# The sums of an expert pass moved from between the gate and the up product to behind the up product

## The reference

```python
def expert_block(args):
    xb, e = args
    h = jax.nn.silu(xb @ w_gate[e]) * (xb @ w_up[e])     # (rows, 1024) @ (1024, 512), twice
    return h @ w_down[e]                                  # (rows, 512) @ (512, 1024)
...
ys = lax.map(expert_block, (xs, blk_exp)).reshape(R, dm)
out = jax.ops.segment_sum(ys * row_w[:, None].astype(ys.dtype), row_tok, num_segments=T + 1)[:T]
x = x + out
```

## Time and profile before

| | |
|---|---|
| median of three runs | 1389.87 us (1386.5 to 1400.7) |
| profiled execution | 1389.18 us, its span 1387.4 us |
| TensorE busy, matmul | 1125.7 us, 81% |
| VectorE, ScalarE, GpSimd busy | 474.2, 174.4 and 22.9 us |
| chain that ended last | TensorE 48%, transfers 41%, VectorE 7% |
| expert stage of layer 0 | 246.6 to 695.3 us |
| expert stage of layer 1 | 922.5 to 1382.9 us |
| mean granted clock of TensorE | 0.905 |

### The profile page before, as it was taken

One profiled execution on the slowest core, in us unless ns is written; L12 is line 12 of the kernel. 1 busy time (PEld: TensorE's weight loads), 2 busy tenths in 40 slices (PEclk: granted clock), 3 DMA queues, 4 the chain that ended last, 5 costly groups with the idle time before them and its releaser, 6 DMA issues.

```text
span 1387.4 us, 23289 instructions
## 1 busy us (share of the span) xinstructions
PE 1125.7 (81%) x9552; PEld 611.2 (44%) x9553; DVE 474.2 (34%) x1245; ACT 174.4 (13%) x415; POOL 22.9 (2%) x35
## 2 busy tenths in 40 slices
PE   5998889998987667777789896999666777779956
PEld 3475545444443333333357564544333333334433
DVE  0873533332232211222158635143221222213311
ACT  2312201010000000000032231100000000000100
POOL 3000000100000000000000000000000000000000
PEclk9998979999999988898999896999988888989988
DMA  9611433889999999999963324339999999995995
GB/s 315 223 62 61 182 121 124 329 359 428 428 428 429 428 428 429 428 428 429 404 246 125 122 69 182 136 141 427 428 428 429 428 428 429 428 428 232 429 429 249
DMA packets 49338, 439.73 MB, mean 317 GB/s; under 512 B 9200, under 2 KB 11408, under 8 KB 24720
## 3 DMA queue, kind: packets, MB, share of 16 engines
q1 hardware_dynamic: 47232, 435.79, 76.1%
q0 software_dynamic: 960, 1.51, 0.6%
q10 hardware_dynamic: 1104, 1.85, 0.4%
HBM read 437.56 MB, written 1.05 MB: 316 GB/s over the span
## 4 chain that ended last, share of the span: by engine, by line
PE 48%; DMA 41%; DVE 7%; issue 2%; DVEq 1%; ACT 1%; ACTq 0%; SPq 0%
DMA ring<-in_e_w_up_dram 19%; DMA ring<-in_e_w_gate_dram 16%; PE PS L1367 12%; PE PS L1415 6%; PE PS L1395 5%; DMA ring<-in_e_w_down_dram 5%; PE PS L1659 4%; PE PS L1339 3%; PE PS L1330 3%; PE PS L1409 2%; PE PS L1349 2%; PE PS L1587 1%; PE PS L1589 1%; PE PS L1678 1%; DMA gT<-in_norm_g_dram 1%
## 5 line engine op out<-in xcount | busy, mean ns | idle before, releaser
L1367 PE MATMUL PS<-ring,hT 128*32 128x256 f32 x4608 | 335.7, 451 | 172.1 <-DMA ring<-in_e_w_gate_dram 120.2
L1367 PEld LDWEIGHTS PS<-ring,hT 128*32 128x32 f32 x4608 | 184.7, 125 | 346.3 <-issue 285.1
L1395 PE MATMUL PS<-ring,hT 128*32 128x512 f32 x1152 | 137.2, 618 | 17.5 <-DMA ring<-in_e_w_down_dram 16.3
L795 DVE TENSOR_SCALAR hT<-hT 128x256 f32<-128x256 f32 x36 | 10.6, 294 | 335.7 <-ACT hT L558 335.7
L1415 PE MATMUL PS<-ring,hT 128*128 128x512 f32 x256 | 121.8, 630 | 0.0
L1339 PE MATMUL PS<-cst,mixT 64*64 64x64 f32 x1216 | 81.6, 283 | 4.5
L1339 PEld LDWEIGHTS PS<-cst,mixT 64*64 64x64 f32 x1216 | 77.4, 213 | 13.5 <-issue 12.0
L1349 PE MATMUL PS<-hT 64*128 64x512 f32 x304 | 75.5, 615 | 1.4 <-ACT hT L563 1.4
L1395 PEld LDWEIGHTS PS<-ring,hT 128*32 128x32 f32 x1152 | 37.4, 113 | 87.9 <-issue 86.4
L1415 PEld LDWEIGHTS PS<-ring,hT 128*128 128x128 f32 x256 | 50.4, 203 | 58.4 <-issue 58.1
L1330 PE MATMUL PS<-xres,scr 128*64 128x512 f32 x304 | 73.6, 605 | 1.8 <-DVE scr L778 1.8
(11 more groups left out here) (335 smaller groups left out, 974.2 us busy)
## 6 DMA issues: line engine op xcount, KB each, us to landing
ring<-in_e_w_gate_dram SPq DMA_DIRECT2D x64, 2048.0 KB, 34.8
ring<-in_e_w_up_dram SPq DMA_DIRECT2D x64, 2048.0 KB, 32.9
ring<-in_e_w_down_dram SPq DMA_DIRECT2D x64, 2048.0 KB, 35.0
ring<-in_w_in_dram SPq DMA_DIRECT2D x10, 2048.0 KB, 18.4
ring<-in_w_out_dram SPq DMA_DIRECT2D x2, 4096.0 KB, 13.6
ring<-in_w_in_dram SPq DMA_DIRECT2D x2, 1024.0 KB, 25.3
xres<-in_x_dram ACTq DMA_DIRECT2D x1, 1024.0 KB, 10.8
out_dram<-xres SPq DMA_DIRECT2D x1, 1024.0 KB, 4.0
```

Source lines behind the costliest of these rows:

```text
L1367: last = pe.matmul(PS[o:o + UT, bank, 0:256], xTe[:, k, UT * u:UT * u + UT], w[u][:, k, :, 2 * h:2 * h + 2], start=k == 0, stop=k == KD - 1)
L1395: last = pe.matmul(PS[o:o + UT, 3, :], hTe[:, c % 2, hc:hc + UT], w[u][:, c, 512 * h:512 * h + 512], start=c == 0, stop=c == KF - 1)
```

## The change

The two lines `combine(n, False)` and `in_product(1, 2)` change places in `one_pass` of TensorE. C is issued behind U and ahead of the gather, in every one of the 36 passes. No other engine's program changes.

```diff
@@ -1370,8 +1370,8 @@
 
                 pe.wait_ge(s_xte, n + 1)
                 in_product(0, 1)
+                in_product(1, 2)
                 combine(n, False)
-                in_product(1, 2)
                 pe.wait_ge(s_hit, n + 1)
                 gather(s_gath)
                 pe.wait_ge(s_h, n + 1)
```

## The result

The changed kernel takes 1393.76 us (median of 20 runs, 1390.01 to 1402.49), the kernel before 1388.20 (median of 20). The ratio is 1.0036 with a 95% interval of 1.0018 to 1.0053: some 5 us slower. Predicted were 1394 and +4.9 us.

A forecast was written before the change was run, and what follows sets the result against it. The prediction took expert weight transfers at 428 GB/s as the bound, with slack on TensorE. Layer 0's end 2.27, layer 1's pause 0.70 and its end 1.92 gave +4.9 us on 1389.18: 1394, range 1388 to 1400.

The forecast's parts named there:

- The bound and the slack: Expert stages: weight transfers at 428 GB/s set the pace; shifts inside transfer-paced passes away from an end are worth 0.
- Release of the up tiles: Up product ends 1.92 us sooner where tiles are there, but both pauses end at a gate product: worth 0.
- Passes with tiles in place: Passes whose tiles are all there: TensorE's work keeps its sum of 17.7 us and nothing is late: worth 0.
- The clock: Up products behind longer bare waits for tiles run partly at 1.2 GHz: taken at 5.36 us, nearly each one slow.
- End of layer 0: Last pass of layer 0: slow up product, then bare combining, start the down product later: +2.27 us.
- End of layer 1: Last pass of layer 1: up product already slow, down product follows without a wait, so combining adds +1.92 us.
- The pause of layer 1: First pass of the twelfth pair, ahead of the transfers' pause: next gate product starts later, +0.70 us.
- The sum: Whole kernel: 2.27 + 0.70 + 1.92 = +4.9 us on a profiled execution of 1389.18 us.
- A (clock no worse): Rival: up products come out no slower by the clock, +1.7 down to -0.9 us, 1388.3 to 1390.9; chance 0.18.
- B: Rival: sooner release of the up tiles shortens the two pauses, at most 1.92 us each, 1390; chance 0.03.
- C: Rival: weight queue runs dry in every pair, 21 gate waits grow, 40 us (1430) or 73 us (1462); chance 0.04.
- D: Rival: the exchange shows nowhere, since the down product waits for its tiles anyway, 1389; chance 0.02.

The follow-up runs named there:

- the block behind U: Changed kernel with four more float32 matmuls of 512 columns behind the combining in every pass, timed against the kernel before: ratio 1.0239, +33 us.
- the wait filled: Changed kernel with seven float32 matmuls of 256 columns between gate and up products in each layer's last pair, against the kernel before: ratio 1.0037.

## Why the prediction was right

**The bound and the slack.** Right. The transfers run on at their rate, each pass takes the late D out of its wait for the gate, and with C behind U in 22 passes the last U's come 0.3 us sooner and 0.6 later than in the mean of before.

**Release of the up tiles, worth 0.** Right. The two pauses in the changed kernel, SP's issues (start, us until the last of the row):

```profile
269.87 20.51 SPq L469 DMA_DIRECT2D ring<-in_e_w_up_dram  x2
...
1224.99 49.37 SPq L469 DMA_DIRECT2D ring<-in_e_w_up_dram  x2
```

They end at 290.38 and 1274.36, again behind the last G of the pair, which began at 286.06 and 1270.05.

**Passes with tiles in place, worth 0.** Right but for some 0.15 us: G and U side by side take less than apart. They stand in one row of 128 matmuls, and the passes follow each other after 17.54 us (17.70 in the earlier trace rows):

```profile
268.52 7.43 PE L1367 MATMUL PS<-ring,hT 128*32 128x256 f32 x128
...
286.06 7.43 PE L1367 MATMUL PS<-ring,hT 128*32 128x256 f32 x128
```

**The clock.** The rule from the rows held: 73 of the 75 U's that waited in the three changed traces were slow; the two quick ones had waited 2.01 and 2.30 us. The line is not sharp: over the traces of before U's behind 2.04 us were slow and one behind 2.44 was quick, and with C behind U in 22 passes one behind 3.93 us was quick. No D was slow in the changed kernel (4, 6 and 7 of 36 before).

The Trainium skill ("TensorE: Matmul & The Clock Gate", "HAM oscillation — how this bites in real kernels") tells this of a kernel whose waits for transfers last some 3 to 5 us: behind each of them the next block starts at the low clock. The slow U's behind 3 us and more in the changed traces agree. The prediction took it for waits of any length, and so read more into it than it states. In the three traces of before 74 U's waited for their tiles: the 37 with 1.99 us or less were all quick, and of the 37 with 2.02 us or more 32 were slow, 27 of them behind 2.04 to 2.76 us, which is shorter than the waits that the skill tells of.

**End of layer 0.** +2.27 stood there; means of three 12.35 against 9.78 us: +2.57.

**End of layer 1.** +1.92; 12.40 against 10.28: +2.12. The trace that I had read was the slow one of three (11.17 us from U to D, against 9.71 and 9.97, where U took 3.88 and 5.25), so the U of 6.45 us that I had kept as it was is partly a loss of the change. By what mattered the two ends are alike, C and the slower U; where C was moved in the last pair alone they cost 3.3 and 2.8 us over the means.

**The pause of layer 1.** The one mis-sized term: +0.70. From the U of the first pass to the next G it was 14.84, 14.76 and 13.33 us before, 15.21, 16.67 and 16.57 after: +1.84, and +1.81 up to the last U of the stage. I had put U at 5.36 us; in two of three it took 6.47 and 6.58. The second trace of the changed kernel:

```profile
1234.01 6.58 PE L1367 MATMUL PS<-ring,hT 128*32 128x256 f32 x64 [5.93 <-DMA ring<-in_e_w_up_dram]
...
1247.23 3.64 PE L1395 MATMUL PS<-ring,hT 128*32 128x512 f32 x32
1250.68 7.43 PE L1367 MATMUL PS<-ring,hT 128*32 128x256 f32 x128
```

Its G had been quick (3.85 us), so the wait to the tiles, which come 9.8 us after G's start, was the longer: the time that a quick G saves, U pays. I had also counted the D of 4.95 us as always slow; in the third trace of before it took 3.43.

**The sum.** +4.9 predicted; the stages of three traces each give +6.8 (2.6 + 2.1 + 1.8, and 0.3 up to the last U of layer 0, where one changed trace lost 1.2 us), the medians +5.6, the ratio +5.0. That the forecast of the median came so near has some luck in it: one term was too small, and the rest of the program scatters more than the error.

**Rivals.** A (clock no worse) fell with the slow U's, B with the pauses that end at a gate product, C with the block behind U, which cost 23 us and not 76, D with U to D.

## What to carry to other kernels

Work that an engine does while it waits for a transfer is free only on that side of the wait. To price moving it, look not at the passes in the middle, which take it in, but at the last pass of each stage and at the passes ahead of each place where the queue of transfers runs empty. A longer idle time of TensorE has a second price, the products behind it at the low clock, and moving the idle time elsewhere moves that price along: it should stand ahead of the product that the end depends on least. And cut traces at the stages before comparing totals: here the parts that nothing touched scattered by more than the effect.

## What the runs showed of the hardware

The stretch ahead of the first G took from 244.06 to 250.94 us over thirteen traces, the one between the stages 230.02 to 237.28, with the same instructions. The same 25 us of the mixer part of layer 0, first in the kernel before, then in the changed one (windows as above):

```profile
140.00:165.00 25.00, 22.66 (x120) 15.90 (x118) 13.98 (x28) 9.89 (x34) 0.00 (x0) 1.00 0.63 237
```

```profile
140.00:165.00 25.00, 25.00 (x102) 17.94 (x100) 10.76 (x23) 8.69 (x30) 0.00 (x0) 0.73 0.52 191
```

TensorE is busy all through in the second, does less (102 records for 120), and is granted 0.73 of its clock in place of 1.00. The same window parts all thirteen traces: in the six with 250.43 to 250.94 us up to the first G the granted clock is 0.73 there and TensorE has 102 to 104 records, in the seven with 244.06 to 246.59 us it is 0.98 to 1.00 with 115 to 120 records. The stretch between the stages goes the same way. In the 20 us that begin 120 us behind the last C of layer 0 the granted clock is 1.00, with 94 to 97 records, in the nine traces in which the stretch took 230.02 to 231.73 us, and 0.75 to 0.77, with 70 records, in the four in which it took 236.81 to 237.28 (C back ahead of U in the last pair, the second block, 22 passes, the wait filled). So each of the two stretches loses 5 us or more in one piece, by the clock.

That all three changed traces had the long first stretch and all three of before the short one can't come from an instruction ahead of it, as none differs. Nor does it follow C: with C moved in part of the passes it fell on both sides (246.49 and 246.25, 250.66), with C behind U in every pass and the wait ahead of U filled in the last pair it was the shortest of all (244.06), and with C ahead of U and the gather beside it it was long (250.60). Why the clock falls there in some executions and not in others stays open.

C's eight records took 1.92 us, a block of eight with 128 rows and as many columns 3.63. C's matmuls come in pairs, one on the upper and one on the lower 64 rows of the array; that the two of a pair run side by side is read from this ratio and wasn't tested by itself.
